# Conditioning steps two in a slot instead of one: a stick-breaking and gated-linear attention layer on one core

## The reference

```
mod = (jax.nn.silu(c) @ w_ada + b_ada)[:, None, :]
sh1, sc1, gt1, sh2, sc2, gt2 = jnp.split(mod, N_MOD, axis=-1)
h = rmsnorm(x, g_pre_mix) * (1.0 + sc1) + sh1
m, k_rows, v_rows, s_new = token_mixer(h, ...)
x = x + gt1 * rmsnorm(m, g_post_mix)
h = rmsnorm(x, g_pre_ffn) * (1.0 + sc2) + sh2
f = (jax.nn.silu(h @ w_ffn_gate) * (h @ w_ffn_up)) @ w_ffn_down
x = x + gt2 * rmsnorm(f, g_post_ffn)
```

## Time and profile before

| | us |
|---|---|
| median of three runs | 1504.8 (1504.07 to 1504.97) |
| span of the profiled execution | 1501.4 |
| the profiled execution's own time | not given apart from the three runs |
| TensorE busy | 1439.7 (96%) |
| VectorE busy | 913.3 (61%) |
| ScalarE busy | 660.7 (44%) |
| 512 instructions of steps 0 to 63 (L1841) | 66.5 busy, 2.2 idle before |

### The profile page before, as it was taken

The page is one execution under the profiler, slowest core; times in us unless marked ns, Lnnn a source line. Parts: engine busy times, 40 slices in busy tenths (PEclk is TensorE's granted clock), DMA queues, the critical chain, the costliest instruction groups (busy, mean ns, idle before and its releaser), DMA issues.

```text
span 1501.4 us, 29221 instructions
## 1 busy us (share of the span) xinstructions
PE 1439.7 (96%) x11274; PEld 1274.0 (85%) x11274; DVE 913.3 (61%) x1501; ACT 660.7 (44%) x1277; POOL 105.2 (7%) x205
## 2 busy tenths in 40 slices
PE   7779999998899999998999999999999999999997
PEld 2247787887568787796899999999999999999997
DVE  2243588995687666457657666566665665446444
ACT  1023477776655544336434434444344343334333
POOL 1000311112322200100000000000000000200000
PEclk9979999999899999999999999999999999999999
DMA  9999999999999978996766565665656555855552
GB/s 370 421 362 360 389 387 402 369 333 397 385 373 326 338 259 281 393 328 257 264 184 182 168 193 172 184 179 168 194 177 185 177 171 186 235 182 181 178 179 94
DMA packets 139043, 396.56 MB, mean 264 GB/s; under 512 B 13130, under 2 KB 17393, under 8 KB 126145
## 3 DMA queue, kind: packets, MB, share of 16 engines
q1 hardware_dynamic: 117730, 319.39, 62.9%
q0 software_dynamic: 21232, 76.10, 13.4%
HBM read 382.14 MB, written 11.21 MB: 262 GB/s over the span
## 4 chain that ended last, share of the span: by engine, by line
PE 80%; DMA 12%; DVE 3%; ACT 2%; issue 1%; POOLq 0%; SPq 0%; POOL 0%; DVEq 0%; ACTq 0%
PE ps L1907 23%; PE ps L1908 23%; PE ps L1909 23%; PE ps L1841 4%; DMA ada_s<-in_w_ada 3%; DMA raw<-in_w_in 2%; DMA v_page<-in_cache_v 2%; DMA k_page<-in_cache_k 2%; DMA ada_r<-in_w_ada 2%; PE ps L2039 2%; DMA x_keep<-x_t 1%; PE ps L1965 1%; DVE k_page L1275 1%; DMA k_page<-in_cache_v 1%; PE ps L1884 1%
## 5 line engine op out<-in xcount | busy, mean ns | idle before, releaser
L1907 PE MATMUL ps<-h_hi,w_hi 128*128 128x264 f32 x2304 | 665.7, 289 | 7.6 <-DVE h_lo L1213 3.6
L1908 PE MATMUL ps<-h_lo,w_hi 128*128 128x264 f32 x2304 | 656.5, 285 | 0.0
L1909 PE MATMUL ps<-h_hi,w_lo 128*128 128x264 f32 x2304 | 655.9, 285 | 0.0
L1907 PEld LDWEIGHTS ps<-h_hi,w_hi 128*128 128x128 f32 x2304 | 435.9, 189 | 53.4 <-issue 38.3
L1729 DVE TENSOR_TENSOR w_lo<-raw,w_hi 128x1024 fp32r<-128x1024 f32 x256 | 309.5, 1213 | 275.4 <-ACT w_hi L1018 274.1
L1018 ACT ACTIVATE w_hi<-raw 128x1024 fp32r<-128x1024 f32 x264 | 278.4, 1059 | 405.0 <-PE ps L1909 393.9
L1908 PEld LDWEIGHTS ps<-h_lo,w_hi 128*128 128x128 f32 x2304 | 435.3, 189 | 0.1
L1909 PEld LDWEIGHTS ps<-h_hi,w_lo 128*128 128x128 f32 x2304 | 434.2, 188 | 0.0
L1225 DVE TENSOR_TENSOR w_lo<-raw,w_hi 128x1024 fp32r<-128x1024 f32 x136 | 166.2, 1223 | 162.4 <-ACT w_hi L702 155.1
L702 ACT ACTIVATE w_hi<-raw 128x1024 fp32r<-128x1024 f32 x128 | 134.9, 1055 | 193.4 <-PE ps L1909 162.4
L1908 PE MATMUL ps<-act_lo,w_hi 128*128 (+1 forms) x704 | 200.4, 285 | 0.0
(11 more groups left out here) (336 smaller groups left out, 1211.6 us busy)
## 6 DMA issues: line engine op xcount, KB each, us to landing
ada_r<-in_w_ada SPq DMA_DIRECT2D x64, 1024.0 KB, 9.4
raw<-in_w_in SPq DMA_DIRECT2D x96, 512.0 KB, 8.3
raw<-in_w_ffn_gate SPq DMA_DIRECT2D x88, 512.0 KB, 3.7
raw<-in_w_ffn_up SPq DMA_DIRECT2D x88, 512.0 KB, 3.8
raw<-in_w_ffn_down SPq DMA_DIRECT2D x88, 512.0 KB, 4.1
ada_s<-in_w_ada SPq DMA_DIRECT2D x32, 1024.0 KB, 13.2
k_page<-in_cache_k POOLq DMA_DIRECT2D x64, 512.0 KB, 7.5
v_page<-in_cache_v POOLq DMA_DIRECT2D x38, 512.0 KB, 7.7
```

The lines of the kernel that those rows point to most:

```text
L1907: mm(out, w_hi, xh, start=first, stop=False)
L1908: mm(out, w_hi, xl, start=False, stop=False)
L1909: return mm(out, w_lo, xh, start=False, stop=last)
```

## The change

The step table puts an even step into the slot of the odd one behind it: steps 0 to 15 in twos in slots 4, 6, 8, 10, 13, 15, 17, 19; 16 to 31 in twos in every fourth slot from 27 to 55; 32 to 47 in slots 97 (two), 98 (one), 101, 103, 105, 107 (two each), 111 (three) and 114 (two). In the first feed-forward group two steps run behind units 0, 2 and 4. SP's places for the loads are derived from the same table by the same rules.

```
-        A_SLOT = {n: 3 + 9 * n // 8 for n in range(16)}
-        A_SLOT.update({16 + k: 25 + 2 * k for k in range(16)})
+        A_SLOT = {n: 3 + 9 * (n | 1) // 8 for n in range(16)}
+        A_SLOT.update({16 + k: 25 + 2 * (k | 1) for k in range(16)})
         A_SLOT.update({32 + k: s for k, s in enumerate(
-            (96, 97, 98, 100, 101, 102, 103, 104, 105, 106, 107, 108, 110, 111, 112, 114))})
+            (97, 97, 98, 101, 101, 103, 103, 105, 105, 107, 107, 111, 111, 111, 114, 114))})
...
-        A_AT = {s: n for n, s in A_SLOT.items()}
+        A_AT = {s: [n for n in sorted(A_SLOT) if A_SLOT[n] == s] for s in A_SLOT.values()}
...
-                if st in A_AT:
-                    ada_next(A_AT[st])
+                for n in A_AT.get(st, ()):
+                    ada_next(n)
...
-                    if first and u < 6:
+                    if first and u in (0, 2, 4):
                         ada_next(58 + u)
+                        ada_next(59 + u)
```

## The result

| | before | after |
|---|---|---|
| median of 7 runs each, us | 1504.07 (1500.94 to 1507.69) | 1509.4 (1508.3 to 1510.45) |
| ratio | | 1.0035 (95%: 1.0025 to 1.0045) |
| span of the profiled execution | 1501.4 | 1508.8 |

The change makes the kernel 0.35% slower, some 5.3 us. The forecast was 1.4 us faster, and the result lies outside its range.

A forecast was written before the change was run, and what follows sets the result against it. TensorE was taken as the bound, except in slots 20 to 35, where a transfer chain sets the time. Terms 1.0 + 0.65 + 0.1 - 0.4 = 1.4 us less gave 1503.4 us, range 1499.5 to 1506.6.

The forecast's parts named there:

- a negative difference at slot 35: Test at the unit after slot 35, expected about 1 us earlier; forecast wrong if the gain was negative or above 2.5 us.
- The price of a further step (0.86): On TensorE, each step after the first in a group of steps costs 0.86 us.
- A lone step before fp32 work: Where fp32 work follows the step, as in slot 53: the step costs 0.99 us and merging it saves 0.13.
- Rival 1: All 27 merges pay in full, 0.33 us each: 9.0 us faster, 1495.8; chance 0.10.
- Slots 4 to 19: First merges, steps 0 to 15: 1.2 us earlier at slot 20, after 0.86 lost on step 0, free in slot 3.
- what passes through: Slots 20 to 35, bound by a transfer chain: of the 1.2 us gained before, 1.0 is kept; bounds 0 and 1.2.
- load 21 was already the last in the queue: Slots 20 to 35: step 21's load lands with the same bytes before it, so three merges there save nothing.
- I cost that at nothing: POOL's first key pages start about 2 us later, but use starts some 10 us on: no cost; 2 us without that cover.
- Rival 3: Transfers run dry as loads 18 and 20 are deferred before slots 31 and 35: 4.9 us slower, 1509.7; chance 0.11.
- Slots 56 to 95 have no step: In these slots the value-page waits move with what precedes, transfers are not full, and nothing changes: 0 us.
- The covers: Slots 96 and 100: steps that filled waits for VectorE's `rstd_rows` move past them and are paid again, 2 x 0.86 = 1.72 lost.
- about half a microsecond of slack by the landing order; no charge: Slots 111 and 114: after the group of three and the pair, step 47's load still lands in time, costing nothing.

The follow-up runs named there:

- e2: Kernel before with only steps 16 to 31 in twos (slots 27 to 55); median 1505.83 us, ratio 1.0014.
- e6: Kernel before with only steps 22 to 31 in twos (slots 39 to 55); ratio 1.0004.
- e1: Kernel before with only steps 0 to 15 in twos (slots 4 to 19); median 1503.79 us, ratio 0.9999.
- e9: Kernel before with five merges among steps 32 to 47 (slots 98, 102, 105, 107, 112), steps 32 and 35 kept in slots 96 and 100; 1506.2 us, ratio 1.0013.
- e8: As e3, but the three in slot 111 become a pair in slot 110 and one step in 111, sending step 47's load one slot earlier; ratio 1.0010.
- e3: Kernel before with only steps 32 to 47 in groups (slots 97 to 114); median 1505.99 us, ratio 1.0016.
- e7: As e3, but step 35 stays in slot 100 and step 36 stands alone in slot 101; ratio 1.0002.
- e10: As e9, plus steps 0 to 15 in twos except 0 and 1 alone, and steps 62 and 63 together; median 1505.35 us, ratio 1.0004.

## Why the prediction was wrong

Three terms that stood at nothing, or near it, failed: the pages that VectorE waits for in slots 20 to 35, the value pages in slots 56 to 75, and in slots 96 to 114 the clock and the load of step 47. The prediction's own sign of being wrong, a negative difference at slot 35, came true: without the start, unit 36 begins 1.0 us later than before.

**What held.** The price of a further step (0.86) and of a lone one between units (1.19) held. Slots 96 and 100 wait as said. In the feed-forward group steps 59 and 61 wait, start to start, 0.8 and 0.56 us for 0.85 and 0.5 forecast:

```profile
721.33 1.07 PE L1841 MATMUL ps<-ada_r,c_t_keep 128*32 128x512 f32 x8 [0.60 <-DMA ada_r<-in_w_ada]
...
729.77 1.07 PE L1841 MATMUL ps<-ada_r,c_t_keep 128*32 128x512 f32 x8 [0.35 <-DMA ada_r<-in_w_ada]
```

**A lone step before fp32 work, "0.99", and its merge, "0.13": mis-sized.** Slots 36 to 55 gained 1.43 us for five merges where 0.65 was said (1.1 us in `e2` and `e6`). In slot 37, with the step gone, the fp32 instruction starts 0.12 us after the last unit matmul:

```profile
261.53 0.28 PE L1909 MATMUL ps<-h_hi,w_lo 128*128 128x264 f32 x1
261.65 1.95 PE L1965 MATMUL ps<-tree 128*128 128x128 f32 x16
```

I had read 0.21 off slot 28, where the next instruction uses 40 rows of the array, and had put it down to fp32. It belongs to the change of shape. Four of the five merges stood before full-array work and saved 0.29 to 0.34 us each. The fifth, out of slot 49, stood before a 40-row instruction as in slot 28, and saved 0.16, near the forecast. After the change it reads:

```profile
315.81 0.28 PE L1909 MATMUL ps<-h_hi,w_lo 128*128 128x264 f32 x1
316.02 0.49 PE L1949 MATMUL ps<-q_rows,pick_rows 40*128 40x512 f32 x1
```

The Trainium skill (TensorEngine Tiling (Array Packing), Key Properties) says that a change of tiling mode drains TensorE. The trace agrees, with 0.12 us from full array to full array and 0.21 into 32 columns or 40 rows. Rival 1's price of 0.33 for a merge was so right wherever full-array work stood on both sides; its 27 x 0.33 fell by all the other terms.

**Slots 4 to 19: the number came out by luck.** 1.14 us were gained where 1.2 was said, but two errors cancel. `e1`, with the same table here, gained 1.72, as the merges are worth more than costed (the one out of slot 16, put at 0.13, stands before a unit and saved 0.35). In the changed kernel step 5, in slot 8, waits for its load, 0.56 us start to start, which the forecast did not have:

```profile
142.42 1.06 PE L1841 MATMUL ps<-ada_r,c_t_keep 128*32 128x512 f32 x8 [0.36 <-DMA ada_r<-in_w_ada]
```

**Slots 20 to 35, "what passes through": wrong sign.** +2.1 instead of +0.2. The step said "load 21 was already the last in the queue" and looked at bytes in front of 249.12. It did not ask who else waits on pages in between. VectorE does: 3.35 us for one key page, and unit 32 then waits 3.3 us for `w_lo`. The late start of the key pages ("I cost that at nothing") was part of it: the first page left 3.5 us later against unit 20, not 2. Rival 3 named the place and the deferred loads, but not the mechanism: the share in 200 to 220 us did not fall below 0.9, it was 1.01. Its 1509.7 is near the result by accident: it put 5.2 us of loss here, where 2.1 stood, and more than half of the loss came from elsewhere.

**"Slots 56 to 95 have no step", "Nothing changes": wrong, +2.9.** TensorE comes to the value pages earlier by what slots 37 to 55 gained, and waits for them. The row of before in slot 57, the changed kernel's, and that of `e2`, which came to unit 56 0.7 us sooner than before:

```profile
357.10 1.07 PE L2039 MATMUL ps<-v_page,a_dec 128*32 128x512 f32 x8 [1.16 <-DMA v_page<-in_cache_v]
```

```profile
359.53 1.07 PE L2039 MATMUL ps<-v_page,a_dec 128*32 128x512 f32 x8 [2.26 <-DMA v_page<-in_cache_v]
```

```profile
359.30 1.94 PE L2039 MATMUL ps<-v_page,a_dec 128*32 128x512 f32 x8 [4.09 <-DMA v_page<-in_cache_v]
```

The eight profiles with pairs in slots 39 to 55 lose 0.5 to 3.0 us in this stretch, 1.85 in the mean; the eleven without any pair in slots 27 to 55 gain 0.45 in the mean (-2.6 to +1.1). That is 2.3 us, more than the 1.4 gained. Slot 57 alone tells the two groups apart: it takes 1.1 to 3.8 us longer than in before in each of the eight, and -0.3 to +0.9 in each of the eleven. The rest fits the loads of steps 30 and 31 leaving as 2 MB in front of the first value pages, but no run separates it. In the changed kernel's own profile slot 57 has 1.1 of the 2.95 us. Behind it stand the longer wait for `q_bcast` and a unit 66 that took 1.85 us longer, at low clock, behind a wait of 2.80 us for a value page; units 61 and 65, slow in before, ran faster. These are not traced to the change: unit 66 is slow in `e9` too, which has no pairs ahead of it.

**Slots 96 to 114: two missing terms.** The covers came out as reckoned, and the six merges saved 1.98 us where 1.78 was said. Missing was the clock behind a longer wait (1.5 us). And step 47, given "about half a microsecond of slack by the landing order; no charge", was 1.7 us late: read from a landing order, not from a landing time moved by the same slots as the step before it in its tile.

## What to carry to other kernels

Moving work out of a wait can cost twice: its own time, and whatever the longer pause does to TensorE's clock. Where loads are ordered by when their buffer is used, a step that moves one slot later moves the next load of its buffer as well; price every merge from the landing of the load two or three places on, and look up in the tile table which step that load hangs on. And time gained in front of a stretch that waits for transfers may not be kept: five merges won 1.4 us in one stretch and lost it in the next.

## What I had not expected of the hardware

**The clock can fall behind a pause of about 2 us.** In 20 profiles, measured from the last start before the pause to the first one after it: slot 100 paused 2.16 us in seven kernels, and unit 101 ran at 1.2 GHz for 3.4 us in all seven; it paused 1.47 us in the 13 others, and in none. Slot 96 paused 2.19 us in eight; unit 97 was slow in four of them, and in none of the twelve with 1.04 us. The same pause thus drops the clock in one execution and not in the other (unit 97 in `e8`, not in `e3`, whose program is the same up to there), at a price of 1.5 us a unit.

**Low clock comes and goes with the same program.** Unit 32 took 3.4 to 5.2 us in 12 of the 20 profiles, among them `e7` and `e8`, whose program up to there is that of before, and 2.9 in the others. How much of that reaches the end is not shown. In `e1` and `e10` unit 32 took 1.1 and 1.5 us longer than in before, and slot 33, where TensorE waits for a step's load, 0.9 and 1.4 less. That such drops make part of the 7 us between the quickest and the slowest run of before is likely, but runs without a profile don't show it.
